# Two halves of a weight split planned apart, and operand tiles set 272 elements apart

## Time and profile before

| | us |
|---|---|
| median of three runs | 2014.66 |
| the profiled execution's own time | 2014.4 |
| its span (first to last instruction) | 2013.1 |
| TensorE matmul busy | 1972.3 |
| VectorE busy | 1158.5 |
| ScalarE busy | 875.0 |
| GpSimd busy | 291.5 |
| DMA, mean rate over the span | 171 GB/s |

### The profile page before, as it was taken

How to read it: one execution, slowest core, us unless ns; L and a number is a source line. 1 busy time by engine, 2 the same in 40 slices (tenths; PEclk the granted TensorE clock), 3 DMA queues, 4 the chain that set the end, 5 groups by cost and what they waited for, 6 DMA issues and landing times.

```text
span 2013.1 us, 37092 instructions
## 1 busy us (share of the span) xinstructions
PE 1972.3 (98%) x15786; PEld 1936.3 (96%) x15786; DVE 1158.5 (58%) x1707; ACT 875.0 (43%) x1264; POOL 291.5 (14%) x320
## 2 busy tenths in 40 slices
PE   7999999999999999999999999999999999999999
PEld 6999999999999999999999989999999999999987
DVE  5765656555554445654554564576456676564644
ACT  5544454444444334444444443446443333444443
POOL 2110010202010002300112242030011132020200
PEclk9999999999999999999999999999999999999999
DMA  7465445455555555555565564443554443556564
GB/s 243 138 191 175 152 152 157 153 179 182 184 183 181 187 186 180 179 187 181 188 220 179 165 200 137 138 146 105 157 179 137 127 135 126 179 184 189 183 230 157
DMA packets 175647, 343.79 MB, mean 171 GB/s; under 512 B 10478, under 2 KB 19050, under 8 KB 174954
## 3 DMA queue, kind: packets, MB, share of 16 engines
q1 hardware_dynamic: 174106, 337.16, 53.0%
q10 hardware_dynamic: 1376, 4.26, 0.6%
HBM read 335.09 MB, written 6.29 MB: 170 GB/s over the span
## 4 chain that ended last, share of the span: by engine, by line
PE 84%; issue 5%; DVE 3%; ACT 2%; POOL 2%; POOLq 0%; ACTq 0%; DVEq 0%
PE bank L1256 83%; ACT w_hi L1581 1%; DVE w_lo L1884 1%; POOL arena L2479 1%; DVE arena L2155 1%; POOL scratch L2476 0%; POOL acc_b L2497 0%; POOL arena L2516 0%; POOL stats L2425 0%; DVE arena L2261 0%; DVE best L2259 0%; DVE scratch L1986 0%; ACT arena L1687 0%; PE bank L1463 0%; DVE arena L2204 0%
## 5 line engine op out<-in xcount | busy, mean ns | idle before, releaser
L1884 DVE TENSOR_TENSOR w_lo<-w_raw,w_hi 128x1024 fp32r<-128x1024 f32 (+2 forms) x644 | 784.6, 1222 | 794.2 <-ACT w_hi L1581 792.9
L1581 ACT ACTIVATE w_hi<-w_raw 128x1024 fp32r<-128x1024 f32 (+2 forms) x644 | 661.4, 1031 | 903.8 <-PE bank L1256 900.6
L1256 PE MATMUL bank<-hb_hi,w_hi 128*128 128x256 f32 x2448 | 701.1, 286 | 0.1
L1256 PE MATMUL bank<-hb_lo,w_hi 128*128 128x256 f32 x2448 | 694.8, 284 | 0.0
L1256 PE MATMUL bank<-hb_hi,w_lo 128*128 128x256 f32 x2448 | 694.8, 284 | 0.0
L1256 PE MATMUL bank<-ob_hi,w_hi 128*128 128x256 f32 (+1 forms) x2224 | 647.7, 291 | 7.0 <-DVE w_lo L1884 4.3
L1256 PE MATMUL bank<-ob_hi,w_lo 128*128 128x256 f32 (+1 forms) x2224 | 628.7, 283 | 0.0
L1256 PE MATMUL bank<-ob_lo,w_hi 128*128 128x256 f32 (+1 forms) x2224 | 627.6, 282 | 0.0
L1256 PEld LDWEIGHTS bank<-hb_hi,w_hi 128*128 128x128 f32 x2448 | 471.2, 192 | 2.4 <-DVE w_lo L1884 1.6
L1256 PEld LDWEIGHTS bank<-hb_lo,w_hi 128*128 128x128 f32 x2448 | 471.3, 193 | 0.4
L1256 PEld LDWEIGHTS bank<-hb_hi,w_lo 128*128 128x128 f32 x2448 | 471.2, 192 | 0.0
(11 more groups left out here) (242 smaller groups left out, 1206.6 us busy)
## 6 DMA issues: line engine op xcount, KB each, us to landing
w_raw<-in_w_in SPq DMA_DIRECT2D x436, 512.0 KB, 3.5
w_raw<-in_w_out SPq DMA_DIRECT2D x64, 512.0 KB, 4.1
w_raw<-in_w_o_conv SPq DMA_DIRECT2D x32, 512.0 KB, 3.6
w_raw<-in_w_o_mla SPq DMA_DIRECT2D x32, 512.0 KB, 3.7
w_raw<-in_w_branch SPq DMA_DIRECT2D x32, 512.0 KB, 3.5
w_raw<-in_w_kv_b SPq DMA_DIRECT2D x16, 512.0 KB, 3.7
w_raw<-in_w_q_b SPq DMA_DIRECT2D x16, 384.0 KB, 3.2
arena<-x_kept SPq DMA_DIRECT2D x2, 2048.0 KB, 9.7
```

Of the source, the lines that this page charges most:

```text
L1256: return nc.tensor.matmul(dst, lhsT, rhs, start=start, stop=stop, skip_group_check=True)
L1581: act(dst, src, ACT.Copy).then_inc(S_("w_hi"), 1)
L1884: tt(low, src, high.bitcast(F32), ALU.subtract).then_inc(S_("w_lo"), 1)
```

## The change

The split of a unit becomes two steps. The high part (ScalarE) stays where the split was; the low part (VectorE) and the load of the w_raw buffer that it frees are planned in the middle of the next unit's tiles (`m == len(u.tiles) // 2`), or, if a unit is about to run whose low part is still unplanned, right before its tiles. hb_hi and hb_lo are allocated with 272 columns per tile, of which the first 256 are used. kr1's own buffer goes, and kr1 becomes a piece of the arena; its evacuation waits in addition for the copy of x to DRAM and for the squares of x.

```diff
@@ plan_work
-    issued = {"load": 0, "split": 0}
+    issued, lows = {"load": 0, "split": 0}, deque()
...
-            plan.split[i] = add("split", i, marks="w_hi w_lo " * (2 if units[i].phase.pairs else 1), free=old)
+            plan.high[i] = add("split_hi", i, marks="w_hi " * (2 if units[i].phase.pairs else 1), free=old)
+            lows.append(i)
+
+    def split_low():
+        while lows:
+            i = lows.popleft()
+            plan.split[i] = add("split_lo", i, marks="w_lo " * (2 if units[i].phase.pairs else 1))
             load()
@@ run
             split_to(i + LEAD)
             u = units[i]
+            if i in lows:
+                split_low()
             for m, tile in enumerate(u.tiles):
                 if u.k0 == 0:
                     out[m] = out[m - 1] if two and m % 2 else banks.take()
                 last = m == len(u.tiles) - 1
+                if m == len(u.tiles) // 2:
+                    split_low()
                 s = add("tile", i, m, bank=out[m], marks="proj" if u.last else "used" if last else "")
@@ Memory
-        self.hb_hi, self.hb_lo = sb("hb_hi", [P, KT, S], F32R), sb("hb_lo", [P, KT, S], F32R)
+        self.hb_hi, self.hb_lo = (sb(n, [P, KT, T], F32R)[:, :, 0:S] for n in ("hb_hi", "hb_lo"))
...
-        self.kr1 = sb("kr1", [P, S])[:, :]
...
+        self.kr1 = r(68, 1, S)
@@ scalar_engine
-    def split(s):
+    def split_hi(s):
@@ vector_engine
-    def split(s):
+    def split_lo(s):
...
-            ve.wait_ge(*s.nth("w_hi", j))
+            ve.wait_ge(*plan.high[i].nth("w_hi", j))
             tt(low, src, high.bitcast(F32), ALU.subtract).then_inc(S_("w_lo"), 1)
...
     def kr(s):
-        out_by(s, m.kr1, m.R, done["r1"])
+        out_by(s, m.kr1, m.R, done["r1"], done["x_kept"], done["x_sq"])
```

More of the change, by code:

```diff
@@ L153, in __init__ @@
         self.sem, self.count, self.steps, self.done, self.split, self.used = sem, {}, [], {}, {}, {}
+        self.high = {}
     def add(self, kind, *args, marks="", dma="", **of):
@@ L1848, in x1_turn @@
             ACT.Copy).then_inc(S_("x1_turned"), 1)
-    does = dict(first_loads=first_loads, split=split, constants=constants, x_tile=x_tile, x_keep=x_keep, sine=sine,
+    does = dict(first_loads=first_loads, split_hi=split_hi, constants=constants, x_tile=x_tile, x_keep=x_keep, sine=sine,
                 bounds_exp=bounds_exp, meta_turn=meta_turn, latent=latent, latent_split=latent_split, v=v,
@@ L2375, in out2 @@
         tt(m.OT[:, blk, w], m.proj[s.of["pb"]], m.OT[:, blk, w], ALU.add).then_inc(S_("evac"), 1)
-    does = dict(clear_halves=clear_halves, split=split, constants=constants, zero_rows=zero_rows, pre_cols=pre_cols, x_tile=x_tile, x_lo=x_lo,
+    does = dict(clear_halves=clear_halves, split_lo=split_lo, constants=constants, zero_rows=zero_rows, pre_cols=pre_cols, x_tile=x_tile, x_lo=x_lo,
                 row_sum=row_sum, factor_out=factor_out, cols=cols, angle=angle, turns=turns, angle_rest=angle_rest,
```

## The result

The changed kernel takes **1978.42 us** (median of 1978.16 to 1979.02), beside 2014.9 for the kernel before, timed with it: ratio 0.9819 [0.9802, 0.9836], 36 us less. Forecast were 1992.5 us and a range from 1984 to 2006, so the sign and both mechanisms were right and the gain was put too small, outside the range. The profiled execution took 1978.3 us, its span 1977.0.

A forecast was written before the change was run, and what follows sets the result against it. TensorE's matmuls, busy 1972.3 of 2013.1 us, were taken to bound the kernel, leaving their pace and TensorE's few waits. Terms -9.1 - 4.4 - 3.7 - 5.0 - 1.7 + 2.0 = -21.9 took 2014.4 to 1992.5 us, range 1984 to 2006.

The forecast's parts named there:

- both mechanisms: Wider hb tile spacing quickens the matmul pace; low parts moved to mid-unit remove TensorE waits. Both gains together: chance 0.72.
- Spacing, -9.1: 7344 matmuls on hb go from 120.0 to oconv's 118.76 ns each: 9.1 us off.
- four places in turn: ob tiles, 1088 bytes apart, begin at four places within 256 bytes; hb's all at one; taken as the pace difference.
- Rival 1: The hb spacing does nothing, as the skill's column-count rule would give: 2001.6 us, chance 0.10.
- Start, -4.4: Phase qa: +1.9 later first low part, -1.6 small waits, -3.0 wait for squares (acc_b), -1.7 half clock.
- qi, -3.7: Phase qi: x1 steps ahead of the low part for units 375 to 378, 1.8 us lost instead of 5.5.
- fb, -2.0 and -1.7: At 1357.83, TensorE's 2.55 us wait for L2235 shrinks by 2.0; the half-clock stretch behind it goes, 1.7.
- Side jobs in the recurrence, -3.0: TensorE's two waits for recurrence step L2345, 3.0 us together, both go with the step ahead of the low part.
- the waits on GpSimd: Two further TensorE waits, on GpSimd, stay where they are in the forecast's sum.
- New waits, +2.0: Low parts now waiting behind softmax steps and evacuations cost 2.0 us at places not seen; bounds 0 and +8.
- the leads: Low parts are ready ahead of TensorE, 4 to 7 us in layer-two phases, so the later order causes little waiting.

The follow-up runs named there:

- e1: Kernel before, with only the change's 272-element hb tiles and kr1 in the arena, split still one step: 2007.24 us.
- e2: Changed kernel with hb tiles 256 elements apart again: 1986.84 us.
- e3: Changed kernel with hb tiles 256 elements apart, all beginning at 64 bytes within 256: 1967.29 us.
- e4: Changed kernel with hb in columns 16 to 272 of its 272-element tiles: 1970.32 us.
- e11: Changed kernel with hb tiles 256 elements apart, all beginning at 128 bytes within 256: 1979.01 us.
- e14: Changed kernel with hb tiles 256 elements apart, all at 192 bytes within 256, weights at 0: 1946.83 us.
- e12: Run e3 with the w_hi and w_lo buffers also moved 64 bytes on: 1988.06 us.
- e16: Changed kernel with hb tiles 256 elements apart at 0 and the w_hi and w_lo buffers at 192 bytes: 1968.09 us.
- e7: Changed kernel with the low part back at the unit's head for the first three splits and phase qa: 1982.98 us.
- e9: Changed kernel with the low part back at the unit's head in phase qi: 1982.03 us.
- e6: Changed kernel with the low part back at the unit's head in phase fb: 1982.84 us.
- e5: Changed kernel with the low part back at the unit's head in phases ga, za and ba: 1989.52 us.
- e17: Run e14 with q, kv, oconv and omla reading ob's buffer as 256-element tiles from 192 bytes on: 1934.99 us.
- the four undoings: Runs e5, e6, e7 and e9, each putting the changed kernel's low part back in some phases: +11.1, +4.4, +4.6 and +3.6 us.
- e18: Run e17 with the first low part planned after x tile 3 and 7 filler matmuls between the layers: 1933.29 us.
- e13: Changed kernel with 15 filler matmuls, 4 and 11, in TensorE's two waits between the layers: 1978.21 us.

## Why the prediction was too small, step by step

**Spacing, -9.1: right.** e1 gives -7.4, e2 8.4, and the pace is 118.75 ns as carried over from oconv. The reasoning "the same work in all but this" held. Its picture of four places in turn was not wrong but not the point: at a fixed distance of 192 the same matmuls go at 113.3. That a pace measured in one phase on ob holds in the phases on hb was in part luck: by e3, e4, e11 and e14 oconv itself can go at 118.2.

Rival 1 named a rule of the Trainium skill (TensorE: Matmul & The Clock Gate, "Back-to-back issue gap"). The formula N/2.4 + 2.5 ns is given there for an isolated matmul, so the 109 ns at 256 columns should not have been held against this stream. For a stream of weight loads and matmuls the section says that both set the spacing, and gives some 81 ns at 128 columns and 131 at 512. The traces go beyond that: at one count of 256 they have 113.3 to 120.0 ns by where the operands lie, and the 512-column matmuls of wout2 start 231.7 ns apart, not 131. The Trainium skill's SBUF — State Buffer, "A bandwidth-pool intuition that's wrong (but worth ruling out)", has a second independent read port for TensorE's weight loads. If the two were independent in all respects, where weights lie should not matter to the stream, and e12 and e16 show that it does. Which part they share the runs do not say.

**Start, -4.4: right** in sum and in parts: first unit 14.84 for a forecast of 14.4, the wait for acc_b and the half clock gone, -4.4 between the traces, e7 +4.6 (4.1 in its trace).

**qi, -3.7: right.** 3.6 by the traces and by e9; 23.1 us for seven units where "about 22" stood.

**fb, -2.0 and -1.7: nearly.** 4.4 (e6), 5.0 between the traces: the stretch costs 1.5 rather than 1.7, and 3.4 of waiting goes rather than 2.0. The stretch costs less than half its length because the stream does not run twice as fast without it: matmuls start 213 ns apart at half clock and 118 to 120 at full.

**Side jobs in the recurrence, -3.0: this step failed.** It took two rows of one name, TensorE's waits on L2345, and measured are 11.1 us (e5) or 12.0 between the traces. From start to start in the same matmuls of both, these two waits are 3.5 us, so they were priced about right; what was left out is the rest. The recurrence is a chain over VectorE, GpSimd and TensorE, and a VectorE step that stands behind a low part delays whichever engine comes next. Three waits on GpSimd (POOL stats, 0.64 each) went, 1.9 us, and two waits at other places (L2319 and one that the profile puts down to no one), 1.6; short ones are 1.0 more. The forecast had let the waits on GpSimd stay. For the one on the arena (2.5 us to 1.0) that is in effect what came: the new wait on L2365 takes its gain back. Secondly the half-clock stretches in these phases, at 1587.2 and 1686.2, followed such waits as the one at 1358 did, but only that was priced; one stood in a bound, the other nowhere. They cost 1.5 us each, together 3.0. Waits 8.0, clock 3.0 and the spacing 0.5 make 11.5 of the 12.0 us.

**New waits, +2.0: did not come.** Outside the start the wait for low parts is 2.4 us, all in qi, less than the 4.3 before, so the leads that the forecast went by sufficed. At e14's faster pace such waits begin to show (0.41 us at 823.40).

**The sum.** 8 us of the 14 missed are the recurrence (11.1 for 3.0), 2 the waits that did not come, 0.7 fb, and about 3 to 4 are small waits in other phases, the difference between e2's 27.8 and the 23.7 of the four undoings. No experiment undid them, but the traces of before and e2 place them: kva is 0.9 shorter and q 0.7 (a wait on GpSimd each), zmla 0.6, wout 0.6, and gconv, gmla and cin3 0.2 each, 3.4 in all. None of them had a term. The bounds were too narrow in the same way: with every one at its best the forecast's terms give 2014.4 - 33.9 = 1980.5 us, still above the 1978.4 measured, and the range began higher, at 1984.

## What to carry to other kernels

When one engine's in-order queue holds a long wait ahead of a side job's steps, price the gain by all of TensorE's waits in those phases plus what each low-clock stretch behind them costs (here 1.5 us of its 3.4), not by the wait rows that carry the job's name: the chain crosses engines, and its delay shows under other names. In these phases TensorE's idle time before, 8.3 us, and two stretches would have given 11.3 for the 11 to 12 measured. That is an upper estimate from one kernel, since a wait can come back under another name, and it came so close because idle time understates each wait a little. Charge a low-clock stretch only where TensorE is what holds the phase; between the layers 10.2 us of it cost 1.1. And if two phases of the same matmuls differ by a nanosecond, try where the two operands' tiles begin relative to each other, and read the pace in every phase: here that was 8 us in the change and 43 more in e17, with the same number of instructions.

## What was not expected of the hardware

- With 256 columns at 2.4 GHz the matmul stream ran at 113.3 to 120.0 ns, depending on the distance of the two operands' places within 256 bytes: 120.0 at 0 and 96, mostly 118.7 at 128, mostly 117.8 at 64, mostly 113.3 at 192. At the last three a second pace was seen too (120.0, 113.3, 117.8), with nothing moved.
- A half-clock stretch of 3.4 us cost 1.5 us in the recurrence phases (e5: the same 17 matmuls in 3.39 us and 1.88), and next to nothing between the layers (e17, e18).
- A plain float32 matmul of 256 columns appears as two records (e13: 11 as x22 in 4.92 us, 4 as x8 in 1.98). The seven more take 2.94 us, 0.42 each, where a float32r one takes 0.12 of the stream at full clock.
